# Order of the high and low weight products in the up columns of a hybrid decoder trunk

## What is computed

```
x = x + 0.5 * swiglu(rmsnorm(x, ffn1_norm[l]), w_gate, w_up, w_down)
...                                   # mixing: projection, two attentions, w_o
x = x + 0.5 * swiglu(rmsnorm(x, ffn2_norm[l]), w_gate, w_up, w_down)

swiglu(t) = (silu(t @ w_gate) * (t @ w_up)) @ w_down      # 1024 -> 2816 -> 1024
```

## Time and profile before

| | |
|---|---|
| median of 3 runs | 937.5 us (937.45 to 937.7) |
| profiled execution | 938.08 us, its span 936.3 us |
| granted TensorE clock | 1.000 (the 2.4 GHz level) |
| TensorE matmul busy | 922.1 us (98%), 4970 matmuls |
| TensorE weight load busy | 784.4 us (84%), 4970 loads |
| VectorE busy | 627.2 us (67%) |
| ScalarE busy | 535.3 us (57%) |
| wide products of the up columns (line 1366) | 1280, mean record 391 ns, busy 318.9 us |
| narrow products of the up columns (line 1373) | 1280, mean record 283 ns, busy 178.8 us |

### The profile page before, as it was taken

One profiled execution on the slowest core, in us unless ns is written; L12 is line 12 of the kernel. 1 busy time (PEld: TensorE's weight loads), 2 busy tenths in 40 slices (PEclk: granted clock), 3 DMA queues, 4 the chain that ended last, 5 costly groups with the idle time before them and its releaser, 6 DMA issues.

```text
span 936.3 us, 14782 instructions
## 1 busy us (share of the span) xinstructions
PE 922.1 (98%) x4970; PEld 784.4 (84%) x4970; DVE 627.2 (67%) x955; ACT 535.3 (57%) x1056; POOL 67.2 (7%) x139
## 2 busy tenths in 40 slices
PE   7999999999999999999999999999999999999998
PEld 5888888888788888888888888888887888888887
DVE  5766666686787666666676666666868776666663
ACT  7655554566875555554555555555679565555551
POOL 4000000023220000000020000000322100000000
PEclk9999999999999999999999999999999999999999
DMA  8855556551064755555557655565601566555541
GB/s 290 260 190 188 193 183 198 179 183 66 23 223 150 250 188 185 196 186 195 180 161 237 194 187 186 194 187 177 199 1 60 197 211 209 192 188 191 190 157 46
DMA packets 45814, 165.43 MB, mean 177 GB/s; under 512 B 5296, under 2 KB 5296, under 8 KB 45776
## 3 DMA queue, kind: packets, MB, share of 16 engines
q1 hardware_dynamic: 44496, 160.98, 52.5%
q0 software_dynamic: 992, 3.42, 1.1%
q10 hardware_dynamic: 288, 0.54, 0.1%
HBM read 163.86 MB, written 1.05 MB: 176 GB/s over the span
## 4 chain that ended last, share of the span: by engine, by line
PE 92%; ACT 3%; DVE 1%; DMA 1%; issue 1%; POOL 0%; DVEq 0%; SPq 0%
PE UV L1366 31%; PE UV L1373 16%; PE A L1303 11%; PE A L1306 11%; PE A L1307 11%; PE UV L1303 2%; PE UV L1307 2%; PE UV L1306 2%; PE UV L1628 1%; ACT work L772 1%; DMA raw<-stream 1%; PE UV L1318 1%; PE UV L1609 1%; PE A L1595 0%; ACT gain L772 0%
## 5 line engine op out<-in xcount | busy, mean ns | idle before, releaser
L887 DVE TENSOR_TENSOR wlo<-raw,whi 128x1024 fp32r<-128x1024 f32 x304 | 370.6, 1225 | 128.1 <-ACT whi L539 127.9
L539 ACT ACTIVATE whi<-raw 128x1024 fp32r<-128x1024 f32 x304 | 317.3, 1052 | 12.5 <-DMA raw<-stream 12.4
L1366 PE MATMUL UV<-acts,whi 128*128 128x512 f32 x1280 | 318.9, 391 | 0.0
L1366 PEld LDWEIGHTS UV<-acts,whi 128*128 128x128 f32 x1280 | 234.9, 188 | 46.8 <-DVE wlo L887 1.5
L1373 PEld LDWEIGHTS UV<-acts,wlo 128*128 128x128 f32 x1280 | 174.3, 190 | 12.1
L1373 PE MATMUL UV<-acts,wlo 128*128 128x256 f32 x1280 | 178.8, 283 | 0.0
L1303 PE MATMUL A<-whi,ht_hi 128*128 128x512 f32 x352 | 138.2, 392 | 0.0
L1306 PE MATMUL A<-wlo,ht_hi 128*128 128x512 f32 x352 | 137.9, 392 | 0.0
L1307 PE MATMUL A<-whi,ht_lo 128*128 128x512 f32 x352 | 137.0, 389 | 0.0
L614 ACT ACTIVATE ht_hi<-work 128x256 fp32r<-128x256 f32 x80 | 33.5, 419 | 121.9 <-DVE work L978 121.9
L610 ACT ACTIVATE work<-UV 128x256 f32<-128x256 f32 x80 | 30.7, 384 | 88.6 <-PE UV L1373 88.6
(11 more groups left out here) (217 smaller groups left out, 847.2 us busy)
## 6 DMA issues: line engine op xcount, KB each, us to landing
raw<-stream SPq DMA_DIRECT2D x304, 512.0 KB, 3.4
gain<-norm_gains POOLq DMA_DIRECT2D x5, 512.0 KB, 6.0
out<-x SPq DMA_DIRECT2D x4, 256.0 KB, 2.0
sgain<-small_gains POOLq DMA_DIRECT2D x2, 324.0 KB, 4.2
x<-x_in SPq DMA_DIRECT2D x1, 512.0 KB, 3.5
x<-x_in ACTq DMA_DIRECT2D x1, 512.0 KB, 7.6
cs<-rope POOLq DMA_DIRECT2D x1, 128.0 KB, 5.6
cgain<-col_gains POOLq DMA_DIRECT2D x2, 1.0 KB, 4.1
```

What stands on the lines that cost most here:

```text
L539: act.activation(whi_half(unit, half), raw[:, n % RAW, :], ACT.Copy).then_inc(hi_done, 1)
L887: dve.tensor_tensor(wlo_half(unit, half), raw[:, n % RAW, :], whi_half(unit, half).bitcast(F32), ALU.subtract).then_inc(split_done, 1)
L1366: last = pe.matmul(UV[c][:, j, :], whi_half(unit, j)[:, k * P:(k + 1) * P], acts[:, :, k, :], start=k == 0, stop=False, skip_group_check=True)
```

## The change

In `columns` the two loops over k become one. For each slice the 512-column product with `whi` is followed at once by the 256-column product with `wlo` of the same slice. The number of matmuls, of weight loads and of waits and signals is the same; the first wide product still starts the bank and still raises `unit_freed`, the last narrow one still ends the group and raises `block_done`. The hook `amid` (four times in the program) is now called ahead of slice 4, that is after four pairs, and no longer between the wide and the narrow products.

```diff
                 half_split(unit, j, i)
                 for k in range(KD):
+                    if k == KD // 2 and amid:
+                        amid()
                     last = pe.matmul(UV[c][:, j, :], whi_half(unit, j)[:, k * P:(k + 1) * P], acts[:, :, k, :],
                                      start=k == 0, stop=False, skip_group_check=True)
                     if k == 0 and freed:
                         last.then_inc(unit_freed, freed)
-                if amid:
-                    amid()
-                for k in range(KD):
                     last = pe.matmul(UV[c][:, j, 0:SEQ], wlo_half(unit, j)[:, k * P:(k + 1) * P], act_hi[:, :, k, :],
                                      start=False, stop=k == KD - 1, skip_group_check=True)
                 last.then_inc(block_done, 1)
```

## The result

| | before | after |
|---|---|---|
| median | 937.6 us (937.45 to 937.94, 4 runs) | 944.06 us (943.78 to 944.68, 4 runs) |
| ratio to before | | 1.0069, 95% interval 1.0058 to 1.0081 |
| span of the profiled execution | 936.3 us | 942.8 us |

The kernel became slower by 6.5 us, or 0.7%. The page of after answers to the earlier trace rows. The order is: busy time by engine, the granted clock in 40 slices, the chain that ended last by engine and by line.

A forecast was written before the change was run, and what follows sets the result against it. The prediction took TensorE's matmul stream, busy for 98% of the span, to bound the kernel. Its four parts summed to 0 - 3.2 + 0 + 0 = -3.2 us, against the 937.5 median 934.3 us, range 930.5 to 943.5.

The forecast's parts named there:

- What bounds the kernel: TensorE's matmuls, busy for 98% of the span; only the step from one matmul to the next could change time.
- Part 1, the pairs: In `columns`, 1280 wide-narrow pairs at 0.345 us each would cost what they cost now: 0.
- fits by 0.007 us: A wide product's load, 0.112 us, was said to hide under a narrow step of 0.119 us.
- Part 2, the tail behind a run: Wide steps after each of 160 narrow runs pay 0.02 us, gone in the new order: minus 3.2 us.
- this case among its ends: Only the 80 runs followed by `columns` lose the tail, those followed by `down` keep it: gain 1.6 us.
- Part 3: At the hook, the two transposes' wait for VectorE's product stays covered, by 0.13 and 0.14 us: 0.
- part 4: At a call's end, `block_done` stays on the last narrow product, so ScalarE and VectorE start as late as now: 0.
- The slow rival: In `columns`, the wide step stays slow in all 1280 pairs, 0.006 to 0.009 us each: 942.0 to 945.8; chance 0.30.
- The argument against it: The excess behind a narrow run spreads over five wide steps, so isn't bound to the step right behind the narrow product.
- The two fast rivals: In `columns`, cheaper narrow steps (925.3) or vanishing overheads in an alternating stream (911); chance of faster, under 932: 0.11.
- the first of them: Every narrow product behind a wide one keeps its shorter first step, 1280 x 0.007 = 9.0 us: 925.3; within 0.11.
- The last of them: Alternating sizes remove each step's overhead, 10 ns on 1280 x 2 steps, 26 us: 911; chance 0.02.

The follow-up runs named there:

- narrow384: Kernel after, with the narrow products streaming 384 columns in place of 256 (part of low activations times low weights added): 1011.78 us.
- both_w64: Kernel after, with wide and narrow products each loading 64 weight columns in place of 128 (half of the hidden columns left out): 929.25 us.
- merge16_but_last: Kernel before, with a gate and an up call's 16 wide products, then their 16 narrow ones, except in each feed-forward's last group: 936.57 us, ratio 0.999.
- runs2: Kernel after, reordered to two wide products, then two narrow ones, four times per call: median 936.87 us, ratio to before 0.9990.
- narrow512: Kernel after, with the narrow products streaming 512 columns too (low weights times low activations added): 1071.29 us.
- its mirrored form: Kernel after, reordered to one wide, two narrow, two wide and so on, one wide at the call's end: 936.81 us, ratio to before 0.9989.
- narrow_whi: Kernel after, with the narrow products loading the high part of the weights again in place of the low part: 943.97 us.
- narrow_cols2: Kernel after, with the narrow products summed into the second 256 columns of the bank in place of the first: 944.45 us.
- runs4: Kernel after, reordered to four wide products, then four narrow ones, twice per call: median 941.27 us, ratio to before 1.0038.
- narrow_w64: Kernel after, with only the narrow products loading 64 weight columns in place of 128 (half of their hidden columns left out): 937.67 us.
- the w64 kernels: Kernels loading 64 of 128 weight columns; on after, for wide, narrow, both: 930.66, 937.67, 929.25 us; on before, for wide, both: 939.13, 934.15 us.

## Why the prediction was wrong

It gave 934.3 us, a range of 930.5 to 943.5, and 0.30 for slower; measured were 944.06, 0.6 us past the range's end.

**What bounds the kernel** held. No engine beside TensorE moved, and the whole difference lies in the steps between matmuls.

**Part 1, the pairs, is the step that failed.** It priced a pair at what the same steps cost in runs, since both the load under a wide step and the one under a narrow step had their rows there. Each of the two does occur in before, but not the sequence. In the new order the pair is 0.353, and the change of the pairs is not the 0 of this part but 1280 x 0.0067 (0.3533 from 1.06 us for three pairs, less 0.3467 from 0.2267 + 0.1200) = 8.5 us. That the wide load "fits by 0.007 us" was the wrong question: the narrow step above that load did not grow, the wide step behind it did, by 0.010. In narrow384 the load fits by 0.06 and the wide steps are slow all the same (three from 88.14 to 89.36 take 0.70 us, 0.233 each). The step depends on the number of weight columns too: in both_w64 that number was cut from 128 to 64, and the alternating pair went from 0.353 to 0.340. The Trainium skill (TensorE: Matmul & The Clock Gate, section Part 2: What happens when you issue a matmul) says that loading the next weights takes no read bandwidth from the running matmul. The runs don't show bandwidth. What they show is that the number of weight columns changes the steps even where the load is hidden; whether by the load or by the columns that then multiply, they don't separate.

**Part 2, the tail behind a run, was right as a reading and half wrong as a consequence.** Fewer runs do save: merge16_but_last has 68 fewer and gains 1.2 us, against 1.4 foretold by the 0.02 of this part. But the new order doesn't take the tail away, and half of the saving of 3.2 us was not there. In `down` it stands in full after a single narrow product (1.16 us for five steps). The text had this case among its ends, at 1.6 us for the 80 runs, and did not choose it. With both: 8.5 less 80 x 0.02 = 6.9 us, against 6.5 measured. Nor is a tail a fixed sum per run: behind two narrow products it is over sooner (runs2).

**Part 3 and part 4** held. In the first feed-forward the moved transposes start at 26.42 us, where the prediction had 26.39, without idle time ahead of them. The view of line 1358 names one short wait, which before has too, and no other in front of the transposes:

```profile
its engine sat idle before it (us, times) until:
  DVE work L959: 0.4, 1
```

In before it is 0.3 us, once. It belongs to the first feed-forward's other pair of transposes (at 21.7 us), which the change doesn't touch.

**The rivals.** The slow rival named the mechanism's place and its size: 0.006 to 0.009 us on the wide step of every pair, 942.0 to 945.8. Measured are 944.06, and 0.0067 a pair: 0.010 more on the wide step, a little over its worst value, and 0.003 less on the narrow one, of which it had nothing. It also subtracted 3.2 us for tails, where half stayed. That its total came out right is in part these errors offsetting each other. It had 0.30. The argument against it, that the excess is spread over five steps and so not bound to the step behind a narrow product, was a weak one: a disturbance that needs five wide steps to die out will not die out when the next narrow product comes after one. That argues for the rival, and should have made it the likeliest or moved the range's end to its own, 945.8. The two fast rivals did not come, though the narrow steps did shrink as the first of them had it, from 0.120 to 0.117 on average. The last of them went with the Trainium skill's rule for an isolated gap (the same page, section Back-to-back issue gap): 216 ns for 512 columns. The most even stream that the runs made, narrow512, has 226 ns.

## What to carry to other kernels

A step's price read in a run of equal matmuls holds for that run alone. Where a change alternates sizes, look in the trace for what a change of size leaves behind, and for how many steps, and put a case in which it is paid again each time inside the range; what it comes to must be measured in the sequence itself, since here it was neither paid once nor the same each time. On a stream without idle time a reordering of the same matmuls still moves the time, and several are cheap to try. Here two and two, its mirrored form, and 16 and 16 outside of the last groups beat the kernel before by 0.1%, with intervals that just exclude no change; four and four lost 0.4% and one and one 0.7%.

## What the runs showed of the hardware

The steps of alternating matmuls settle into a pattern that repeats: with 512 and 256 columns and loads of 128 it is three pairs in 1.06 us, and the pair isn't the sum of what its two steps cost in runs. The excess is on the wide step, 0.237 us against 0.226. Fewer weight columns don't make a run of wide matmuls faster: 0.229 us a step with 64 columns loaded against 0.226 with 128. A run of eight narrow products leaves the next five wide steps 0.03 us longer in sum, in `down` as in the up columns, and a single narrow product at the end of an alternating call leaves as much in `down`; behind pairs of narrow products `down` is back at 0.227 a step after three steps. What in TensorE keeps this memory is not settled.

Ruled out are the tensor of the weights (narrow_whi), the columns of the bank (narrow_cols2), and a fixed price per change of width (runs2 against runs4). A load too long for the narrow step is not the only cause: the narrow steps of after are no longer than those of before, and fewer columns in the narrow product's load, which lies under the wide step, take the pair down to 0.347 (narrow_w64). Not separated are the length of a load and the columns of the array and partitions of PSUM that the w64 kernels leave unused. That one width throughout, with loads of 128 columns, has neither price nor tail is shown by narrow512.
